# Gaps between the slots of two rings of split weights, and a shift between the rings

## The reference

```
h = rms_norm(x)
u, dq, dk, dv, sq, sk, sv, fq, fk, fv, f, gate_logits = split(h @ w_in)     # 1024 x 7428
y_n = branch_n(...) @ w_branch[rows of n]                                   # 1280 rows in all
x = x + (sum_n sigmoid(gate_n + b_gate_n) * y_n) @ w_out                    # 1024 x 1024
x = x + (silu(g) * up) @ w_down,   g, up = split(rms_norm(x) @ w_up)        # 1024 x 5632, 2816 x 1024
```

## Time and profile before

| | |
|---|---|
| device time, three runs | 861.63, 861.67, 861.88 us; median 861.67 us |
| span of the profiled execution (first to last instruction) | 859.8 us; its own device time is not given beside it |
| median less span | 1.9 us |
| TensorE busy | 855.7 us, 4246 products |
| VectorE, ScalarE, GpSimd busy | 593.9, 446.0, 113.6 us |
| DMA | 160.53 MB, mean 187 GB/s |

### The profile page before, as it was taken

One profiled execution on the slowest core, in us unless ns is written; L12 is line 12 of the kernel. 1 busy time (PEld: TensorE's weight loads), 2 busy tenths in 40 slices (PEclk: granted clock), 3 DMA queues, 4 the chain that ended last, 5 costly groups with the idle time before them and its releaser, 6 DMA issues.

```text
span 859.8 us, 11140 instructions
## 1 busy us (share of the span) xinstructions
PE 855.7 (100%) x4246; PEld 711.6 (83%) x4246; DVE 593.9 (69%) x850; ACT 446.0 (52%) x646; POOL 113.6 (13%) x89
## 2 busy tenths in 40 slices
PE   9999999999999999999999999999999999999998
PEld 7888888888888888888888888888888888888887
DVE  7896967768777665564479768768696765565543
ACT  7567654854454444443364674558443644444431
POOL 0750101005401000000005401010063000000000
PEclk9999999999999999999999999999999999999999
DMA  9846656475657666555566465665665576665641
GB/s 343 290 150 190 200 175 183 148 228 180 188 184 236 190 195 190 182 185 189 162 186 178 119 195 158 196 197 162 205 196 179 151 234 183 185 190 177 195 147 50
DMA packets 87815, 160.53 MB, mean 187 GB/s; under 512 B 7505, under 2 KB 14161, under 8 KB 87761
## 3 DMA queue, kind: packets, MB, share of 16 engines
q1 hardware_dynamic: 87328, 159.16, 58.8%
q10 hardware_dynamic: 432, 0.66, 0.2%
HBM read 158.74 MB, written 1.05 MB: 186 GB/s over the span
## 4 chain that ended last, share of the span: by engine, by line
PE 93%; DVE 3%; DMA 2%; ACT 1%; SPq 1%; issue 0%; ACTq 0%
PE bulk L1692 28%; PE bulk L1696 28%; PE bulk L1693 28%; DMA raw<-in_w_in_dram 2%; DVE w_lo L1013 2%; PE bankAB L1432 1%; PE bankAB L1634 1%; PE bankT L1587 0%; PE bankAB L1576 0%; ACT w_hi L737 0%; PE bankAB L1441 0%; PE bankAB L1532 0%; PE bankO L1545 0%; PE bankT L1634 0%; PE bankO L1634 0%
## 5 line engine op out<-in xcount | busy, mean ns | idle before, releaser
L1013 DVE TENSOR_TENSOR w_lo<-raw,w_hi 128x1024 fp32r<-128x1024 f32 (+1 forms) x288 | 362.3, 1272 | 156.5 <-ACT w_hi L737 152.9
L737 ACT ACTIVATE w_hi<-raw 128x1024 fp32r<-128x1024 f32 (+1 forms) x286 | 297.7, 1049 | 245.3 <-PE bulk L1696 240.8
L1692 PE MATMUL bulk<-w_hi,hT_hi 128*128 128x512 f32 (+1 forms) x880 | 344.1, 391 | 0.2 <-DVE w_lo L1013 0.2
L1693 PE MATMUL bulk<-w_lo,hT_hi 128*128 128x512 f32 (+1 forms) x880 | 339.2, 385 | 0.0
L1696 PE MATMUL bulk<-w_hi,hT_lo 128*128 128x512 f32 (+1 forms) x880 | 336.5, 386 | 0.0
L1692 PEld LDWEIGHTS bulk<-w_hi,hT_hi 128*128 128x128 f32 x880 | 165.3, 188 | 33.2 <-DVE w_lo L1013 0.7
L1696 PEld LDWEIGHTS bulk<-w_hi,hT_lo 128*128 128x128 f32 x880 | 165.0, 188 | 33.4
L1693 PEld LDWEIGHTS bulk<-w_lo,hT_hi 128*128 128x128 f32 x880 | 165.4, 188 | 31.7
L1692 PE MATMUL bulk<-w_hi,aT_hi 128*128 128x512 f32 x174 | 68.0, 391 | 0.0
L1696 PE MATMUL bulk<-w_hi,aT_lo 128*128 128x512 f32 x174 | 67.7, 389 | 0.0
L1693 PE MATMUL bulk<-w_lo,aT_hi 128*128 128x512 f32 x174 | 67.7, 389 | 0.0
(11 more groups left out here) (259 smaller groups left out, 720.7 us busy)
## 6 DMA issues: line engine op xcount, KB each, us to landing
raw<-in_w_in_dram SPq DMA_DIRECT2D x110, 512.0 KB, 4.1
raw<-in_w_ffn_up_dram SPq DMA_DIRECT2D x80, 512.0 KB, 4.4
raw<-in_w_ffn_down_dram SPq DMA_DIRECT2D x44, 512.0 KB, 3.3
raw<-in_w_branch_dram SPq DMA_DIRECT2D x20, 512.0 KB, 4.2
raw<-in_w_out_dram SPq DMA_DIRECT2D x16, 512.0 KB, 3.4
bias<-in_b_gate_dram SPq DMA_DIRECT2D x16, 256.0 KB, 4.4
raw<-in_w_ffn_up_dram SPq DMA_DIRECT2D x16, 256.0 KB, 3.2
raw<-in_w_in_dram SPq DMA_DIRECT2D x10, 256.0 KB, 2.7
```

The lines of the kernel that those rows point to most:

```text
L737: act.activation(w_hi[:, g % RING, :, 0:width], raw[:, g % RAW, :, 0:width], ACT.Copy).then_inc(hi_ready, 1)
L1013: vec.tensor_tensor(w_lo[:, g % RING, :, 0:width], raw[:, g % RAW, :, 0:width], w_hi[:, g % RING, :, 0:width].bitcast(F32), ALU.subtract). ...
L1692: pe.matmul(dst, hi, whi, start=(k == ks[0]), stop=False)
L1693: pe.matmul(dst, hi, wlo, start=False, stop=False)
```

## The change

The two rings become one allocation. A k tile takes 520 elements instead of 512 (2080 bytes: 2048 and a gap of 32), and the second ring begins 2 x 5 x 520 + 4 elements (20816 bytes) after the first. A k tile with number n = 2 x slot + i (0 to 9) thus starts 32n bytes past a multiple of 2048 in `w_hi`, and 336 + 32n bytes past one in `w_lo`. 336 is 10 x 32 + 16: the gaps of the first ring and 16 more. The views that engines use keep their shape (slot, k tile, 512 columns); a slot is now two runs of 512 elements and not one of 1024.

`raw`, `hT` and `aT` stay aligned to 2048 bytes. `oT` and `queries` are aligned to 128 bytes. No instruction, wait or semaphore is added or taken away.

```diff
-        w_hi = sb("w_hi", [P, RING, 2, NC], F32R, align=LINE)
-        w_lo = sb("w_lo", [P, RING, 2, NC], F32R, align=LINE)
+        pitch = NC + 8
+        split = sb("split", [P, 4 * RING * pitch + 4], F32R, align=LINE)
+        w_hi, w_lo = (split[:, at:at + 2 * RING * pitch].rearrange("p (s i n) -> p s i n", s=RING, i=2)[:, :, :, 0:NC]
+                      for at in (0, 2 * RING * pitch + 4))
...
-        oT = [sb("oT_hi", [P, 10, SEQ], F32R, mixing, LINE), sb("oT_lo", [P, 10, SEQ], F32R, mixing, LINE)]
+        oT = [sb("oT_hi", [P, 10, SEQ], F32R, mixing, 128), sb("oT_lo", [P, 10, SEQ], F32R, mixing, 128)]
...
-        queries = [sb(f"queries_{part}", [P, 4, SEQ], F32R, mixing, LINE) for part in ("hi", "lo")]
+        queries = [sb(f"queries_{part}", [P, 4, SEQ], F32R, mixing, 128) for part in ("hi", "lo")]
```

## The result

The changed kernel takes 878.53 us (median of three runs, 878.26 to 878.72), before 861.67 us: ratio 1.0194, 95% interval 1.018 to 1.0208. It is 16.9 us slower. The forecast was 868.9 us with a range of 846 to 878: the sign was right, the amount less than half, and the range ended half a microsecond short.

What follows compares the result with a forecast made beforehand. The prediction took the kernel as bound by the number of products times TensorE's pace of starting them. Span 859.8 + 7.2 = 867.0 us, with 1.9 us from span to median 868.9 us; range 846 to 878 us.

Steps and rivals of the forecast that it cites:

- (a): In both splits: two runs of 512 elements instead of one of 1024 cost nothing, bounds 0 and 0.3 us.
- (b): 240 weight loads read `oT`, moved to other multiples of 128 bytes: taken at nothing, 1.0 us if its products slow.
- (c): In the weight products: the moving operand's phase jumps, half of the products lose 4.3 ns, +7.2 us; chance 0.24.
- the good half: About half of TensorE's start phases within 6.7 ns, those giving 226.7 ns; the 16-byte offset could stay among them.
- the beat: TensorE's settled interval between starts of 512-column products: 226.7 ns, 13.3 ns above the columns alone.
- No product finds the beat again: Rival for the weight products: the phase jumps every time, all lose 4.3 ns, +14.4 us, 876.1 us; chance 0.16.
- Nothing changes: Rival: the overhead depends on when TensorE starts its reads, not where they lie; 861.7 us; chance 0.24.
- The faster rival: Rival: moving stream and weight load take turns where the low ring is 16 bytes off; 849.4 or 825 us; chance 0.36.
- the worst intervals: Upper bound for the weight products: all at the slowest interval seen, 236 ns, +31 us; left out of the range.

Runs made afterwards that it cites:

- `rings_by_32`: The kernel before with both rings moved by 32 bytes as a whole, stationary tiles left where they were: 881.2 us, 1.0227.
- `all_by_32`: The kernel before with the rings and all stationary tiles (hT, oT, queries, keys, aT) moved by the same 32 bytes: 861.85 us, 1.0002.
- Products alone: Kernels of their own, real weights in SBUF, 48 products a stretch, nothing else running, other addresses each stretch: the change's pattern took 232.5 ns a product.

## Why the prediction was right or wrong

**What bounds the kernel: right.** The pace of TensorE decided all; the feeders only waited longer (252.4 and 162.6 us).

**(a) Two runs instead of one, priced at nothing: right** (1284 and 1061 ns).

**(b) `oT` off its lines: taken at nothing, wrong by 1.6 us** as measured alone; the bound that I named for it, 1.0 us at 4.3 ns, had the mechanism and fell short for the same reason as in (c).

**(c) The phase of the moving operand: the mechanism was right in kind, the size was wrong, and this is the step that failed.** I took half of the products at 4.3 ns more, since a step of 32 bytes would throw the stream out and "some three of the six products" would bring it back, and the 16 bytes could stay inside the good half. Both halves of that are refuted. With the gaps alone, 91% of intervals are off the beat and not half of them; with the 16 bytes alone 876.4 us and not 862. The reason is that I let a shifted address act like a shifted start. It does not: with one operand shifted the stream has other steady cycles, so there is in most placements no beat to get back to (moving tiles by 32 held 233.3 ns after ten starts of ten). In the kernel before, all 58 runs of ten or more intervals reach the beat of 226.7, after 0 to 16 intervals, and no other cycle holds; 57 of them stay on it. The rows could not show this, as the tiles of all 512-column products in them lay at multiples of 512 bytes; what could be read from them was that no 512-column product at another phase had ever been seen on the beat.

The second factor was too small as well: 4.3 ns is how far the recovery of the earlier trace rows lies above the beat, 5.3 ns is the difference of the two means. With all products and 5.3 ns the sum would have been 17.7 us.

**The rivals.** "No product finds the beat again" is what happened, with a chance of 0.16 and 876.1 us, 2.4 below the measurement, since it had 4.3 ns in place of 5.3; its reason (recoveries longer than the steps) is not the one shown. "Nothing changes" rested on the four stationary places 512 bytes apart; those are multiples of 256, the step found harmless since. It also had behind it the two independent read ports of the Trainium skill's page "SBUF — State Buffer", section "Who interferes with whom". By that rule the place of the moving tiles would not matter next to that of the stationary ones, and `rings_by_32` against `all_by_32` (881.2 and 861.85 us) says that it does; that the ports themselves are where the two meet is not shown. The faster rival, turns taken by two reads 16 bytes apart, had no support: no stretch of any kernel with 512 columns went under 226.6 ns. The 2.5 ns that the Trainium skill's page "TensorE: Matmul & The Clock Gate", section "Wait — 56ns, not 53.3ns?", adds to the columns hold here for bf16 (215.8 ns) and for no fp32r stream.

**Readings of the rows that did not hold.** The earlier trace rows was read as an overhead at another phase that speaks against the gain. Products alone show that it could not tell: with 384 columns the pace is 173.3 ns with the moving tiles in place and with them 32 bytes further, 13.3 above the columns both times. The transposes of the earlier trace rows were read as a stream at half rate without overhead; 0.11 us fits two streams of 128 columns at full rate as well, and the two records of each fp32 product above leave both open. The 0.66 in the earlier trace rows is the DMAs' share of the stretch and not microseconds. Recoveries of the kernel before took up to 16 intervals and not 12. And a run does not always keep the beat once it has it: the one from 245.59 us of the kernel before, in which only `hT_hi` is multiplied, has five intervals of 226 or 227 ns and then 232, 234, 236 and 228, with no transpose between.

**The range** ended at 878 because I cut it between the case of all products at 4.3 ns and the worst intervals. The case of all products was worth more than 0.16: of the paces off the beat, the rows showed many, and of ways to stay on it at another phase none.

**What stays open:** what TensorE's stream collides with. That the places of both operands and the number of stationary columns change the pace speaks for the weight load as the partner, but the shortest load did not give the shortest interval (32 columns 231.7 ns, 128 columns 226.7, both aligned), and no placement takes the last 13 ns away. A product without a weight load beside it was not tried.

## What to carry to other kernels

If fp32r products of 512 columns are back to back, start the tiles of both operands at multiples of 256 bytes, and don't be content with 32-byte alignment of each: in the whole kernels here 4 to 6 ns of 227 depend on it for each product, 12 to 20 us of 862. Both operands by the same 32, 64 or 128 bytes was as good, by the same 16 or 48 it was not. Gaps against supposed bank conflicts are to be tried on products alone first: 48 in a row gave the mean interval of the kernel after and that of `rings_by_32` to 0.2 ns. One start is not enough, though: for the shift of 112 it promised 226.7 ns where the kernel had 231.1. Trust a placement when every start of several ends in the same pace.

## What the runs showed of the hardware

- Address placement changes the pace of fp32r products without any other engine: 226.7, 228.9, 230.0, 231.1, 233.3 ns for 512 columns are each held to the end of a stretch. bf16 and plain fp32 show nothing of a shift of 32 bytes, and fp32r with 384 columns neither.
- A steady cycle can depend on the start: the same addresses held 226.7 ns twice and 231.1 eight times.
- Fewer columns do not always take less time: 512, 504 and 500 columns have 226.7 ns, 256 columns 120.0 and 260 columns 118.7 (aligned, last 24 intervals). With 256 columns a shift of 32 bytes is a gain, 117.8 ns.
- A weight load of fewer columns is shorter (32 columns 109 ns, 128 columns 188) and yet the products beside it are further apart (231.7 and 226.7 ns).
- No placement tried beats the kernel before, so no version faster than both is proposed.
